# Spreading a norm's factors over the partitions through memory in a two-layer decoder trunk: two feed-forward norms on one Trainium2 core

## The chip, the cores and the metric

The kernel runs on one core of one Trainium2 chip. The metric is the device time of one execution in microseconds, lower is better, and the time of a kernel is the median of its runs. The engines named below are TensorE (PE for its matmuls, PEld for its weight loads), VectorE (DVE), ScalarE (ACT), GpSimd (POOL) and SyncE (SP). Each engine takes its instructions in program order, and the engines wait for one another only through semaphores.

## What is computed

A token stream x of 512 rows by 1024 features passes two layers. Each has a mixer (a convolution and pooling mixer in layer 0, attention in layer 1) and then a gated feed-forward part, which is what matters here:

```python
def rmsnorm(x, g):
    y = x32 * lax.rsqrt(jnp.mean(x32 * x32, axis=-1, keepdims=True) + EPS)
    return y * g
def conv_glu_ffn(xn, w_up, conv_w, conv_b, w_down):
    u = causal_dwconv3(xn @ w_up, conv_w) + conv_b
    gate, up = jnp.split(u, 2, axis=-1)          # 2816 columns each
    return (jax.nn.silu(gate) * up) @ w_down
x = x + conv_glu_ffn(rmsnorm(x, ffn_norm[layer]), ...)
```

The norm gives one factor for each token, `rsqrt(mean + EPS)`.

## The kernel before

**Layout.** Features lie on the 128 partitions and the 512 tokens along the free axis, so that x is 8 tiles of 128 x 512. Each float32 matrix product is made of three passes with the operands split into a rounded part and a rest (`wh`, `wl` for weights, `xh`, `xl` for x). A weight unit of 128 output columns is thus 8 x 3 = 24 matmuls of 128 x 512 (lines 1184 to 1186, in `product`). SP loads each unit from memory into one of four slots `raw`, ACT rounds it to `wh` (L483, `round_unit`, called by `ahead`), POOL subtracts to get `wl` (L448), and PE waits for that (`unit_ready`). ACT may round a unit only when PE is done with the unit four before it (`s_unit`), since they share a slot.

**The norm.** The gain is multiplied in before the product, but the token's factor is only applied after it: PE multiplies the raw x by the weights, and DVE multiplies the result in PSUM by `rstd` (L963), which must hold the 512 factors as a row, the same on all 128 partitions. The factors are made with tokens on partitions: ACT squares, DVE sums the squares into `acc`, four small matmuls (`norm_stats`, L1201) sum over the features and leave the means as a column of 4 values on each of the 128 partitions, and DVE works out the inverse root in twelve tiny steps (L835 to L838) into `small[:, 3, 0:4]`, which raises `s_rn`. Then PE spreads them: four transposes of a column repeated along the free axis (`norm_spread`, L1208) write 128 x 512 into the PSUM bank `nbank`, and ACT copies it to `rstd` (`keep_rstd`, L510), which DVE waits for.

**The order around the feed-forward part.** `first_two` makes units up and up + 1 together, tile of x by tile of x, as the tiles become ready. Then units up + 2 and up + 3 follow, then a loop over the rest, one unit after the other into four PSUM banks in turn; unit up + 4 writes bank 0 again, so PE waits there for DVE's first multiplication (`s_z`). In layer 0 the squares are ready in the midst of `first_two`: the statistics stand before its fifth tile and the spread before its eighth. In layer 1 (`late`) the statistics come after `first_two`, and the spread within unit up + 2, after five of its eight tiles. The DVE and ACT steps for the pair (gate, up) are in `hidden`: L963 for gate and up, L595 and L599 on ACT (scale and bias of the third tap), four fused multiply-adds L970 on DVE, then the silu L605 on ACT. In ACT's program the rounding of unit up + 4 stands between L595 and L599, and that of unit up + 5 right behind the first silu.

The kernel also uses memory as a go-between once already: 16 rows of bias are written by ACT's queue (L564), and each head loads one of them with an overlapping pattern into 128 partitions of 2 KB (L703).

## Time and profile before

| | |
|---|---|
| median of 3 runs | 1115.33 us (1115.22 to 1115.8) |
| the profiled execution's own time | 1115.61 us |
| its span in the trace | 1113.6 us |
| PE busy | 1107.0 us, 99% of the span |
| DVE, ACT, POOL busy | 53%, 45%, 42% |
| granted clock of TensorE | 1.00 |

The busy share of PE is modelled from pipelined matmuls; a stretch without a gap shows more surely in the starts of its matmuls in the timeline. A row of the timeline gives the start, the duration, the engine and line, the operation with its tiles, and in brackets how long the engine had been idle before and what ended that.

### The profile page before, as it was taken

To read this page: it belongs to the slowest core of one execution; us is meant where nothing else is said; L and a number is where in the kernel's file an instruction comes from. 1 tells how busy PE (TensorE), PEld (TensorE's weight loads), DVE (VectorE), ACT (ScalarE), POOL (GpSimd) and SP (SyncE) were. 2 spreads that over 40 slices of the span, in tenths; PEclk is the share of its full clock that TensorE was granted. 3 is DMA by queue.
4 is the path that set the end of the run, shared out by engine and by line. 5 is a ranking of instruction groups with operands and counts; after the bars stand their busy time and mean duration, and the time that the engine had idled before them with its cause. 6 is when DMAs were issued, how large, how long until landed. Compare 5 with 4: busy or idle time off the path is not lost.

```text
span 1113.6 us, 15736 instructions
## 1 busy us (share of the span) xinstructions
PE 1107.0 (99%) x5252; PEld 943.6 (85%) x5252; DVE 585.9 (53%) x1070; ACT 498.8 (45%) x805; POOL 462.6 (42%) x221
## 2 busy tenths in 40 slices
PE   9999999999999999999999999999999999999998
PEld 7788888888888888889999999888888888888887
DVE  6785755454454521125688888887654454540000
ACT  5333444444444423223777777644443444442120
POOL 4454534444445354543223233144544445344442
PEclk9999999999999999999999999999999999999999
DMA  8232313223232233333222333122323232224331
GB/s 270 76 115 86 123 59 112 100 88 113 78 111 85 64 104 100 96 94 118 76 77 76 102 98 95 49 98 91 120 87 113 79 109 94 78 66 116 90 107 72
DMA packets 47125, 108.19 MB, mean 97 GB/s; under 512 B 4272, under 2 KB 19632, under 8 KB 47088
## 3 DMA queue, kind: packets, MB, share of 16 engines
q1 hardware_dynamic: 44752, 103.46, 29.3%
q10 hardware_dynamic: 2336, 4.24, 1.5%
q8 instruction: 22, 0.36, 0.1%
q14 instruction: 15, 0.12, 0.0%
HBM read 105.54 MB, written 2.15 MB: 97 GB/s over the span
## 4 chain that ended last, share of the span: by engine, by line
issue 45%; PE 34%; POOL 20%; DMA 1%; SPq 1%; POOLq 0%; ACT 0%; DVE 0%; DVEq 0%
POOL wl L448 20%; PE bank L1184 7%; PE bank L1186 7%; PE bank L1185 7%; PE spt L1184 4%; PE spt L1186 4%; PE spt L1185 4%; DMA raw<-w_in 1%; SPq L377 0%; POOLq L447 0%; POOLq L453 0%; SPq L384 0%; PE obank L1186 0%; PE obank L1184 0%; PE obank L1185 0%
## 5 line engine op out<-in xcount | busy, mean ns | idle before, releaser
L448 POOL TENSOR_TENSOR wl<-raw,wh 128x1024 fp32r<-128x1024 f32 (+2 forms) x214 | 458.0, 2145 | 626.5 <-ACT wh L483 626.1
L1184 PE MATMUL bank<-xh,wh 128*128 128x512 f32 x800 | 311.9, 390 | 0.0
L1186 PE MATMUL bank<-xh,wl 128*128 128x512 f32 x800 | 311.4, 389 | 0.0
L1185 PE MATMUL bank<-xl,wh 128*128 128x512 f32 x800 | 311.3, 389 | 0.0
L483 ACT ACTIVATE wh<-raw 128x1024 fp32r<-128x1024 f32 (+2 forms) x214 | 201.9, 946 | 152.2 <-PE spt L1186 139.9
L963 DVE TENSOR_TENSOR work<-bank,rstd 128x512 f32<-128x512 f32 x88 | 60.6, 691 | 225.7 <-PE bank L1186 223.7
L1184 PEld LDWEIGHTS bank<-xh,wh 128*128 128x128 f32 x800 | 150.2, 188 | 31.8 <-issue 0.9
L1186 PEld LDWEIGHTS bank<-xh,wl 128*128 128x128 f32 x800 | 150.2, 188 | 31.2
L1185 PEld LDWEIGHTS bank<-xl,wh 128*128 128x128 f32 x800 | 150.2, 188 | 31.1
L1184 PE MATMUL spt<-bh,wh 128*128 128x512 f32 x440 | 171.5, 390 | 0.4 <-POOL wl L448 0.3
L1185 PE MATMUL spt<-bl,wh 128*128 128x512 f32 x440 | 171.3, 389 | 0.0
L1186 PE MATMUL spt<-bh,wl 128*128 128x512 f32 x440 | 171.2, 389 | 0.0
L970 DVE SCALAR_TENSOR_TENSOR work<-work,par 128x512 f32<-128x512 f32 x176 | 127.8, 787 | 2.4 <-ACT work L599 1.8
L935 DVE TENSOR_TENSOR x<-spt,x 128x512 f32 (+1 forms) x27 | 18.6, 690 | 208.0 <-PE spt L1186 208.0
L599 ACT ACTIVATE work<-work,par 128x512 f32<-128x512 f32 x44 | 35.9, 816 | 142.2 <-DVE work L963 142.2
L1184 PEld LDWEIGHTS spt<-bh,wh 128*128 128x128 f32 x440 | 82.6, 188 | 18.3 <-POOL wl L448 0.7
L1186 PEld LDWEIGHTS spt<-bh,wl 128*128 128x128 f32 x440 | 82.6, 188 | 17.1
L1185 PEld LDWEIGHTS spt<-bl,wh 128*128 128x128 f32 x440 | 82.6, 188 | 17.1
L1366 PE MATMUL bank<-wh,xh 128*128 128x384 f32 x256 | 87.6, 342 | 0.1
L1368 PE MATMUL bank<-wh,xl 128*128 128x384 f32 x256 | 85.7, 335 | 0.0
L1367 PE MATMUL bank<-wl,xh 128*128 128x384 f32 x256 | 85.7, 335 | 0.0
L595 ACT ACTIVATE work<-work,par 128x512 f32<-128x512 f32 x44 | 35.9, 817 | 57.6 <-DVE work L963 57.6
(154 smaller groups left out, 1140.8 us busy)
## 6 DMA issues: line engine op xcount, KB each, us to landing
raw<-w_up SPq DMA_DIRECT2D x88, 512.0 KB, 3.2
raw<-w_down SPq DMA_DIRECT2D x32, 384.0 KB, 3.1
raw<-w_qkv SPq DMA_DIRECT2D x32, 384.0 KB, 3.4
raw<-w_down SPq DMA_DIRECT2D x32, 320.0 KB, 2.9
raw<-w_in SPq DMA_DIRECT2D x14, 512.0 KB, 3.7
raw<-w_out SPq DMA_DIRECT2D x8, 512.0 KB, 3.2
work<-bias_rows ACTq DMA_DIRECT2D x16, 256.0 KB, 3.8
raw<-w_o SPq DMA_DIRECT2D x8, 512.0 KB, 3.3
```

What stands on the lines that cost most here:

```text
L448: nc.gpsimd.tensor_tensor(wl[s][:, 0:n], raw[s][:, 0:n], plain(wh[s][:, 0:n]), ALU.subtract).then_inc(s_lo, 1)
L483: nc.scalar.activation(wh[s][:, 0:n], raw[s][:, 0:n], ACT.Copy).then_inc(s_hi, 1)
L595: nc.scalar.activation(ug, zg[j][:, 2:], ACT.Identity, bias=col(i * 16 + (c + 3)), scale=col(i * 16 + (c + 2))).then_inc(s_id, 1)
L599: nc.scalar.activation(uu[j], zu[j][:, 2:], ACT.Identity, bias=col(i * 16 + (c + 7)), scale=col(i * 16 + (c + 6))).then_inc(s_id, 1)
L963: nc.vector.tensor_tensor(buf[:, 2:], bank[2 * j + n][:], rstd[:], ALU.mult).then_inc(s_z, 1)
L970: nc.vector.scalar_tensor_tensor(u, z[:, tap:tap + SEQ], col(i * 16 + (c + 4 * n + tap)), u, ALU.mult, ALU.add).then_inc(done, 1)
L1184: mm(dst, wh[s][:, w], hi, start=first, stop=False)
L1185: mm(dst, wh[s][:, w], lo, start=False, stop=False)
L1186: return mm(dst, wl[s][:, w], hi, start=False, stop=last)
L1366: mm(dst, xh[:, k, rows], pair_weights(wh, k), start=k == 0, stop=False)
L1367: mm(dst, xh[:, k, rows], pair_weights(wl, k), start=False, stop=False)
L1368: return mm(dst, xl[:, k, rows], pair_weights(wh, k), start=False, stop=k == KT - 1)
```

## The change

For the two feed-forward norms, the four transposes on PE and ACT's copy of their result are taken out. In their place ACT's queue writes the 4 x 128 factors to a row of 512 floats in memory (`rstd_rows`), waits until they have landed, and loads that row into all 128 partitions of `rstd`. DVE waits for the load. In ACT's program the rounding of unit up + 4 now stands ahead of these two transfers. The two mixer norms are left as they are.

```diff
+    rstd_rows = nc.dram_tensor("rstd_rows", [2, SEQ], F32, kind="Internal").ap()
...
             def ffn(layer, up, down):
-                keep = layer + 2
+                def send_rstd():
+
+                    act.wait_ge(s_rn, 2 * layer + 2)
+                    row = rstd_rows[layer:layer + 1, :]
+                    act.dma_start(row.rearrange("a (t q) -> (a q) t", q=P), small[:, 3, 0:TB],
+                                  allow_slow_non_contiguous=True).then_inc(s_row, 16)
+                    act.wait_ge(s_row, (layer + 1) * 16)
+                    src = bass.AP(tensor=row.tensor, offset=row.offset, ap=[[0, P], [1, SEQ]])
+                    act.dma_start(rstd[:], src).then_inc(s_rstd_in, 16)
...
                     ahead(up, i, 2 * j)
                     if first:
-                        keep_rstd(keep)
+                        ahead(up, i, 1)
+                        send_rstd()
                     act.wait_ge(s_z, f * 2 + 1)
...
-                    ahead(up, i, 2 * j + 1)
+                    if not first:
+                        ahead(up, i, 2 * j + 1)
...
-                dve.wait_ge(s_rstd, layer + 2)
+                dve.wait_ge(s_rstd_in, (layer + 1) * 16)
...
-                    if not late and k == KT - 1:
-                        norm_spread(norm)
...
                 if late:
                     norm_stats(norm)
-                    unit_ready(up + 2)
-                    up_part(2, 0, 5)
-                    norm_spread(norm)
-                    up_part(2, 5, KT).then_inc(s_unit, 1)
-                else:
-                    project(bank[2][:], up + 2, 2)
+                project(bank[2][:], up + 2, 2)
```

How this moves ACT's program at the start of layer 1's feed-forward part, in the kernel before. The first row is the rounding of unit up + 3, the third of unit up + 4, the last of unit up + 5:

```order
483 L483 ACTIVATE wh<-raw 128x1024 [waits s_unit,s_raw3]
484 L510 ACTIVATE rstd<-spt 128x512 [waits s_bc]
485 L595 ACTIVATE work<-work,par 128x512 [waits s_z]
486 L483 ACTIVATE wh<-raw 128x1024 [waits s_unit,s_raw0]
487 L599 ACTIVATE work<-work,par 128x512 [waits s_z]
488 L605 ACT_TABLE_LOAD
489 L605 ACTIVATE work<-work 128x512 [waits s_t0]
490 L483 ACTIVATE wh<-raw 128x1024 [waits s_unit,s_raw1]
```

The same place in the changed kernel, whose line numbers are a few higher (L486 is the rounding, L607 and L612 are what L595 and L599 were):

```order
484 L486 ACTIVATE wh<-raw 128x1024 [waits s_unit,s_raw3]
485 L486 ACTIVATE wh<-raw 128x1024 [waits s_unit,s_raw0]
486 L590 DMA rstd_rows<-small 128x4x1 [waits s_rn]
487 L594 DMA rstd<-rstd_rows 128x512 [waits s_row]
488 L607 ACTIVATE work<-work,par 128x512 [waits s_z]
489 L612 ACTIVATE work<-work,par 128x512 [waits s_z]
490 L618 ACT_TABLE_LOAD
491 L618 ACTIVATE work<-work 128x512 [waits s_t0]
492 L486 ACTIVATE wh<-raw 128x1024 [waits s_unit,s_raw1]
```

The rounding of unit up + 4 has moved ahead of everything that needs the factors; it now waits only for unit up. That of unit up + 5 still stands behind the silu, and so behind both transfers.

On PE, in layer 1, the kernel before has this in the midst of unit up + 2 (the last three matmuls of its fifth tile, the spread, the first of its sixth):

```order
2269 L1184 MATMUL bank<-xh,wh 128x512
2270 L1185 MATMUL bank<-xl,wh 128x512
2271 L1186 MATMUL bank<-xh,wl 128x512
2272 L1208 MATMUL spt<-par,small 128x128 [waits s_rn]
2273 L1208 MATMUL spt<-par,small 128x128 x3
2274 L1184 MATMUL bank<-xh,wh 128x512
```

In the changed kernel the same place is matmuls alone, and PE no longer waits for `s_rn`:

```order
2267 L1197 MATMUL bank<-xh,wh 128x512
2268 L1198 MATMUL bank<-xl,wh 128x512
2269 L1199 MATMUL bank<-xh,wl 128x512
2270 L1197 MATMUL bank<-xh,wh 128x512
2271 L1198 MATMUL bank<-xl,wh 128x512
```

## Rows read from the trace of the kernel before

**Rows 1.** The page: busy times, and the granted clock in 40 slices
```profile
span 1113.6 us, 15736 instructions
PE 1107.0 (99%) x5252; PEld 943.6 (85%) x5252; DVE 585.9 (53%) x1070; ACT 498.8 (45%) x805; POOL 462.6 (42%) x221
...
PEclk9999999999999999999999999999999999999999
```

**Rows 2.** Waits of PE over the whole span (us in total, times, longest)
```profile
PE bank L1247 <- DVE wh L855: 1.7, 1, 1.7
PE obank L1230 <- DVE gate L846: 0.9, 1, 0.9
PE spt L1184 <- POOL wl L448: 0.3, 1, 0.3
```

**Rows 3.** Timeline of PE, layer 0: the spread, and the starts of three units
```profile
153.89 0.60 PE L1208 MATMUL spt<-par,small 128*128 128x128 f32 x4
154.24 0.48 PE L1184 MATMUL bank<-xh,wh 128*128 128x512 f32 x1
...
161.16 0.39 PE L1184 MATMUL bank<-xh,wh 128*128 128x512 f32 x1
...
166.60 0.39 PE L1184 MATMUL bank<-xh,wh 128*128 128x512 f32 x1
...
172.04 0.39 PE L1184 MATMUL bank<-xh,wh 128*128 128x512 f32 x1
```

**Rows 4.** Timeline of PE, layer 1: unit up's end, spread, three units
```profile
759.69 0.39 PE L1186 MATMUL bank<-xh,wl 128*128 128x512 f32 x1
...
764.94 0.60 PE L1208 MATMUL spt<-par,small 128*128 128x128 f32 x4
...
767.45 0.39 PE L1184 MATMUL bank<-xh,wh 128*128 128x512 f32 x1
...
772.89 0.39 PE L1184 MATMUL bank<-xh,wh 128*128 128x512 f32 x1
...
778.33 0.39 PE L1184 MATMUL bank<-xh,wh 128*128 128x512 f32 x1
```

**Rows 5.** Timeline of ACT, layer 0's first pair
```profile
156.04 0.82 ACT L595 ACTIVATE work<-work,par 128x512 f32<-128x512 f32 x1 [0.92 <-DVE work L963]
```

**Rows 6.** Timeline of DVE: layer 0's first factors; layer 1's roots
```profile
155.32 1.29 DVE L963 TENSOR_TENSOR work<-bank,rstd 128x512 f32<-128x512 f32 x2 [2.60 <-PE bank L1186]
...
761.78 0.17 DVE L805 TENSOR_SCALAR guess<-small 128x4 int32<-128x4 int32 x1
...
763.77 0.17 DVE L838 SCALAR_TENSOR_TENSOR small<-small 128x4 f32<-128x4 f32 x1
...
766.26 1.29 DVE L963 TENSOR_TENSOR work<-bank,rstd 128x512 f32<-128x512 f32 x2 [1.93 <-issue]
```

**Rows 7.** Timeline of POOL: layer 1's unit up + 3, up + 4, up + 5
```profile
758.89 2.38 POOL L448 TENSOR_TENSOR wl<-raw,wh 128x1024 fp32r<-128x1024 f32 x1 [3.52 <-ACT wh L483]
768.83 2.39 POOL L448 TENSOR_TENSOR wl<-raw,wh 128x1024 fp32r<-128x1024 f32 x1 [7.56 <-ACT wh L483]
774.13 5.21 POOL L448 TENSOR_TENSOR wl<-raw,wh 128x1024 fp32r<-128x1024 f32 x2 [2.91 <-ACT wh L483]
```

**Rows 8.** Timelines of DVE and POOL: the attention norm's roots
```profile
513.61 1.70 DVE L805 TENSOR_SCALAR guess<-small 128x4 int32<-128x4 int32 x1
515.35 0.17 DVE L806 TENSOR_SCALAR small<-small 128x4 f32<-128x4 f32 x1
...
509.82 5.47 POOL L448 TENSOR_TENSOR wl<-raw,wh 128x768 fp32r<-128x768 f32 x3 [6.31 <-ACT wh L483]
```

**Rows 9.** Timelines of DVE, ACT, POOL: a later pair that nothing disturbs
```profile
189.77 2.73 DVE L970 SCALAR_TENSOR_TENSOR work<-work,par 128x512 f32<-128x512 f32 x4
...
191.87 0.63 ACT L605 ACTIVATE work<-work 128x512 f32<-128x512 f32 x1 [1.10 <-DVE work L970]
192.41 1.04 ACT L483 ACTIVATE wh<-raw 128x1024 fp32r<-128x1024 f32 x1
...
193.53 2.40 POOL L448 TENSOR_TENSOR wl<-raw,wh 128x1024 fp32r<-128x1024 f32 x1 [5.30 <-ACT wh L483]
```

**Rows 10.** DMA issues: KB each, median us from issue to landing
```profile
raw<-w_down SPq DMA_DIRECT2D x32, 384.0 KB, 3.1
raw<-w_qkv SPq DMA_DIRECT2D x32, 384.0 KB, 3.4
...
raw<-w_in SPq DMA_DIRECT2D x4, 256.0 KB, 5.4
...
bias_rows<-bv_sb ACTq DMA_DIRECT2D x1, 48.0 KB, 1.8
```

**Rows 11.** The sixteen bias loads (L703) alone: issue to landing
```profile
DMA to landing us min/median/max: 3.0/3.8/5.2
```

More of the change, by code:

```diff
@@ L236, in trunk @@
         s_rstd = sem("s_rstd")
+        s_row = sem("s_row")
+        s_rstd_in = sem("s_rstd_in")
         s_small = sem("s_small")
@@ L506, in prep, with keep_rstd @@
                 nc.scalar.activation(sq[:], tile(x, k), ACT.Square).then_inc(s_sq, 1)
-            def keep_rstd(spreads):
-                act.wait_ge(s_bc, spreads)
+            def keep_rstd():
+                act.wait_ge(s_bc, 1)
                 nc.scalar.activation(rstd[:], nbank, ACT.Copy).then_inc(s_rstd, 1)
@@ L548, in _ @@
                 if g == 0:
-                    keep_rstd(1)
+                    keep_rstd()
                 else:
@@ L1202, in norm_stats, with norm_spread @@
                 last.then_inc(s_ms, 1)
-            def norm_spread(norm):
-                pe.wait_ge(s_rn, norm + 1)
+            def norm_spread():
+                pe.wait_ge(s_rn, 1)
                 for b in range(TB):
@@ L1273, in _ @@
             first_end(2)
-            norm_spread(0)
+            norm_spread()
             first_end(3)
@@ L1313, in _ @@
                 project(rbank[n % 2], U_OUT + n, n % RING, bh, bl, MIX)
-            def up_part(j, k0, k1):
-                for k in range(k0, k1):
-                    last = product(bank[j][:], j, k, xh[:, k, :], xl[:, k, :], k == 0, k == KT - 1)
-                return last
             def ffn(layer, up, down):
```

## The prediction

> **What bounds the kernel now.** I read the page first: PE is busy in 1107.0 of 1113.6 us at full granted clock, no other engine above 53% [rows 1]. A busy share of pipelined matmuls proves little, so the list of PE's waits comes next: three waits, 2.9 us in all, two of them at the start, and none in a feed-forward part [rows 2]. Then the starts in PE's timeline: unit up + 3 of layer 0 begins at 161.16, the next at 166.60 and 172.04 [rows 3], that is 24 matmuls in 5.44 us, 227 ns each, and layer 1 shows the same from 767.45 to 772.89 to 778.33 [rows 4]. So the end is set by PE's own instructions in a row. Taking an instruction from PE gives its time back, and any other engine costs nothing until it comes later than PE needs it. The question is how much slack the factors have.
>
> **What is removed.** In layer 0 the spread begins at 153.89 and unit up + 2 begins six matmuls later. Unit up + 2 is one unit of 5.44 ahead of 161.16, so it begins at 155.72; six matmuls take 6 x 0.227 = 1.36, so the spread cost 155.72 - 153.89 - 1.36 = 0.47 us [rows 3]. In layer 1: from the spread at 764.94 to unit up + 3 at 767.45 are nine matmuls, 2.51 - 2.04 = 0.47 us [rows 4]. PE did not wait for `s_rn` at either place. Together **-0.94 us**. ACT's copy goes too; it lies beside PE.
>
> **What is added, and when PE would notice.** Two transfers in a row: W, the write of the factors until it has landed, and R, the load, each from issue to landing. The end of R starts DVE's first multiplication; call that time z. Two things of PE hang on z. Unit up + 4 needs bank 0 free, at z + 0.75. Unit up + 5 needs its weights, whose rounding stands behind the first silu on ACT. The second comes later, worked out so: L595 starts 0.72 behind z (155.32 to 156.04) and takes about 0.8 [rows 5, 6]; L599 follows at z + 1.5 and ends at z + 2.3; of the four fused steps the second needs it, so it and the third take until z + 3.7 at 2.73 / 4 = 0.68 each, and the silu starts at about z + 3.75. From the silu to the rounding is 0.54, from the rounding to POOL's start 1.12, and POOL takes 2.40 [rows 9]. PE can start unit up + 5 at **z + 7.9**. Before, this chain took longer, since POOL's work on unit up + 4 lay in its midst [rows 7]; the moved rounding takes that out of the way, which is why I don't take the old length.
>
> *Layer 0.* The factors are ready long before; ACT reaches the write when unit up is done, 0.47 earlier than DVE's start at 155.32 shows it, so the issue is at about 155.0, right behind the start of the moved rounding. z = 155.0 + W + R + 0.2. PE wants unit up + 5 at 172.04 - 0.47 = 171.57, so z may be as late as 163.7: no stall while W + R is under 8.5 us.
>
> *Layer 1.* Here the statistics come after `first_two`, and the moved rounding does harm. Unit up's last matmul starts at 759.69 and ends near 760.1 [rows 4]; ACT rounds unit up + 4 until 761.3, when POOL has just ended up + 3 (758.89 + 2.38 = 761.27) [rows 7]. POOL starts up + 4 then and holds to 763.7. DVE's twelve tiny steps run in this very time, from 761.6 [rows 6]. What happens is seen at the attention norm: the step L805 took 1.70 us in place of 0.17 and ended when POOL's run ended, 509.82 + 5.47 = 515.29 [rows 8]. So L805 at 761.78 ends at 763.7, not 761.95, and `s_rn` comes 1.76 later than 763.94, at 765.7 [rows 6]. The write goes out at 765.8, z = 766.0 + W + R. PE wants unit up + 5 at 778.33 - 0.47 = 777.86, so z may be 769.96 at most. **The stall is W + R - 3.96.**
>
> *W.* Nothing in the trace writes pieces of four bytes. The lower bound is the one write there is, 16 rows: 1.8 us [rows 10]. `small` holds each factor apart in memory order, so the write is 512 pieces. What pieces cost: the w_qkv load moves the same 384 KB as a w_down load in three pieces for each partition in place of one, and lands after 3.4 in place of 3.1 us [rows 10]. 256 pieces more for 0.3 us make 0.6 for some 500 more: 2.4. The only row with 512 pieces is a first w_in load, 5.4 us in a full queue [rows 10], which is the upper bound. I take 2.5, near the lower, since at that time one weight load at most is in flight.
>
> *R.* The bias loads have its shape, 128 rows of 2 KB from one small region of memory: 3.0 to 5.2, median 3.8 [rows 11]. The weight load that POOL's work on unit up + 4 releases at 763.7 is over when R starts, and the next one waits for unit up + 5, which is what is late; so R has the queues for itself. I take 3.2, near the shortest.
>
> W + R = 5.7, the stall in layer 1 is 1.7 us, and in layer 0 there is none (margin 2.8). The sum is -0.94 + 1.7 = **+0.8 us**. On the profiled execution's own 1115.61 (its span of 1113.6 and 2.0 around it) that is 1116.4; the median of the runs lies 0.28 lower, so I predict **1116.1**. A stall of this length should not cost more than itself: after PE's 1.7 us wait at the start the granted clock still reads full [rows 1, 2].
>
> The Trainium skill, "DMA: Bandwidth & Descriptors", Anatomy of one DMA, gives a fixed cost of about 2.0 us for each transfer plus its bytes over 436 GB/s, most of it the receipt of the write, memory being the slowest target. As an estimate from that page W is 2.0 and R 2.0 + 0.6 = 2.6, so that W + R would be 4.6, the stall 0.6 and the time 1115.0. That formula was fitted on GpSimd's path; the rows here, where the sum uses ACT's queue, lie above it for the load (3.0 at least) and below it for the write (1.8), so the sum goes by the rows. The same page, Rules for kernel authors, says that a last dimension that is not contiguous becomes one descriptor for each element; no run here shows it yet, and the 512 pieces above are counted from the code's strides.
>
> **The rivals.**
>
> 1. *The transfers are hidden, or nearly.* W at the bound 1.8 and R at 3.0 make 4.8: a stall of 0.84, time 1115.2. If besides DVE is not held up by POOL in layer 1, 1.76 goes from the stall and nothing is left: 1114.4. For it: both bounds are measured rows, and layer 0 has slack to spare. Against it: L805 was held up once in just this meeting [rows 8], and four-byte pieces can hardly be faster than rows of 3 KB in their fixed part. The page's formula above falls into this case.
> 2. *Slower than can be told from no change.* One mechanism: the round trip through memory in layer 1 is long, so that unit up + 5's weights come late. It decides from a stall of 3.2 us, W + R over 7.1. With R like the longest bias load, 5.2, and W 3.0, W + R is 8.2, the stall 4.2, and the time 1118.6; with R at the median 3.8 and W 5.4 it is 9.2, layer 0 stalls by 0.7 too, and the time is 1120.3. For it: W is unmeasured and all 128 partitions read the same 2 KB. Against it: the queues are nearly empty there.
> 3. *Faster by over 0.2%.* That needs 2.2 us. The removed work on PE is 0.94 in all, and PE waits for nothing around it [rows 2 to 4], so there is nothing more to gain.
>
> **How the numbers follow.** About 0.2%, 2.2 us, is what a measurement of this kernel can tell from no change: 1113.1 to 1117.5. The forecast (a stall between 0.84 and 3.1 us in layer 1, 1115.2 to 1117.5) has 0.60, rival 1 has 0.18, rival 2 has 0.20, rival 3 has 0.02. Forecast and rival 1 are within the bound, so faster 0.02, same 0.78, slower 0.20. The range runs from rival 1 without any stall, 1114.4, to rival 2's first price, 1118.6.
>
> **What the changed profile would show.** No transposes at the feed-forward norms, and starts of matmuls 227 ns apart through the place of the spread. In layer 0 a write issued near 155.0, z near 160.9, PE without a wait. In layer 1 the step that was L805 stretched to about 1.9 us under POOL, the write issued at 765.8, z at 771.7, POOL's unit up + 5 from about 777.1, and one wait of PE for POOL of about 1.7 us at the start of unit up + 5, none elsewhere. I am wrong if the wait is at bank 0 (then z is not followed by the chain of 7.9), if the write's landing takes over 4 us, if the roots run undisturbed beside POOL, or if PE waits in later pairs as well, which would mean that the lag is carried on rather than made up in DVE's idle time.

## The result, and the profile of the changed kernel

The changed kernel takes **1130.48 us** (median of 4 runs, 1130.01 to 1131.01) against 1115.28 us (1114.93 to 1115.8) for the kernel before on the same chip: 1.0135 times as long, 95% interval 1.0123 to 1.0147, 15.2 us slower. The forecast was 1116.1 with a range to 1118.6.

The page of the changed kernel, its busy line and the granted clock in 40 slices (before: [rows 1]):

```profile
span 1129.0 us, 15721 instructions
...
PE 1111.5 (98%) x5244; PEld 945.4 (84%) x5244; DVE 595.2 (53%) x1070; ACT 498.1 (44%) x803; POOL 463.7 (41%) x221
...
PEclk9999999999999999999999999998999999999999
```

The span is 15.4 us longer although PE has eight instructions fewer. A slice of the clock is below full for the first time, the 28th, which begins 27/40 into the span, at 762 us: layer 1's feed-forward part. PE's waits say where (before: [rows 2]; us in total, times, longest):

```profile
PE bank L1197 <- DVE work L976: 11.9, 2, 7.2
```

Two new waits, one in each layer, both for DVE's first multiplication by the factors (L976), which frees bank 0. In PE's timeline they stand at unit up + 4. Layer 0 (before: [rows 3]), the end of unit up + 3, unit up + 4's first two matmuls, the first that is quick again, and the first of up + 5:

```profile
165.43 0.39 PE L1199 MATMUL bank<-xh,wl 128*128 128x512 f32 x1
170.49 0.79 PE L1197 MATMUL bank<-xh,wh 128*128 128x512 f32 x1 [4.67 <-DVE work L976]
171.07 0.63 PE L1198 MATMUL bank<-xl,wh 128*128 128x512 f32 x1
...
173.52 0.40 PE L1198 MATMUL bank<-xl,wh 128*128 128x512 f32 x1
...
177.52 0.50 PE L1197 MATMUL bank<-xh,wh 128*128 128x512 f32 x1
...
777.80 0.39 PE L1199 MATMUL bank<-xh,wl 128*128 128x512 f32 x1
785.42 0.79 PE L1197 MATMUL bank<-xh,wh 128*128 128x512 f32 x1 [7.24 <-DVE work L976]
786.01 0.63 PE L1198 MATMUL bank<-xl,wh 128*128 128x512 f32 x1
...
791.13 0.43 PE L1198 MATMUL bank<-xl,wh 128*128 128x512 f32 x1
...
793.71 0.39 PE L1197 MATMUL bank<-xh,wh 128*128 128x512 f32 x1
```

The rows from 777.80 on are the same place in layer 1 (before: [rows 4]). Every microsecond is in these rows. After the first matmul behind the wait they start 0.43 us apart where it was 0.227 before, until the spacing returns to 0.23 (from the 8th matmul in layer 0, from the 14th in layer 1). Layer 0 lost 170.49 - (165.43 + 0.23) = 4.83 us waiting, and unit up + 4 took 177.52 - 170.49 = 7.03 us in place of 5.44, 1.59 more. Layer 1 lost 785.42 - 778.03 = 7.39 and 8.29 - 5.44 = 2.85. That is 12.22 of waiting and 4.44 of slow matmuls, 16.66 in all. Against the kernel before, unit up + 5 starts 5.48 us later in layer 0 (177.52 for 172.04) and 15.38 later in layer 1 (793.71 for 778.33), and 15.38 is the whole difference of the spans. So 1.28 us came back elsewhere: 0.94 for the transposes and 0.34 of small shifts. The largest of these is 0.47 us by which this execution was ahead before layer 0's feed-forward part (the statistics' matmuls start at 148.40, before at 148.87).

This is what each stretch took, not what each cause cost. The slow matmuls are for the most part not lost on top: POOL had the weights of unit up + 5 ready only 7.9 us behind DVE's first multiplication, at 177.5 and about 792.5, and at full clock PE would have stood still until then. Measured so, they cost next to nothing in layer 0 (177.52) and 1.2 us in layer 1 (793.71).

What DVE waited for is in ACT's timeline of both places, where the queue's instructions have "ACTq":

```profile
154.38 0.40 ACTq L590 DMA_DIRECT2D rstd_rows<-small  x1
165.50 0.34 ACTq L594 DMA_DIRECT2D rstd<-rstd_rows  x1
170.39 0.81 ACT L607 ACTIVATE work<-work,par 128x512 f32<-128x512 f32 x1 [14.97 <-DVE work L976]
...
771.35 0.38 ACTq L590 DMA_DIRECT2D rstd_rows<-small  x1
779.85 0.34 ACTq L594 DMA_DIRECT2D rstd<-rstd_rows  x1
```

Between the write's issue and the load's lie 11.1 and 8.5 us. The load may only be issued once the write has landed, so this is the write's landing. The trace's list of DMA issues (KB each, median us to landing; before: [rows 10]) has it as the slowest transfer of the kernel, with no more than 2 KB to move:

```profile
raw<-w_up SPq DMA_DIRECT2D x88, 512.0 KB, 3.3
...
rstd<-rstd_rows ACTq DMA_DIRECT2D x2, 256.0 KB, 4.4
...
bias_rows<-bv_sb ACTq DMA_DIRECT2D x1, 48.0 KB, 1.8
rstd_rows<-small ACTq DMA_DIRECT2D x2, 2.0 KB, 9.8
```

The same view over 154.3 to 166 us alone, 40 slices of 0.29 us (share of the 16 DMA engines in tenths, and GB/s), then packets by queue and landings:

```profile
DMA  0003400000000000340000005631901430202350
GB/s 0 0 0 3 4 0 0 0 0 0 0 0 0 0 0 0 84 140 0 0 0 0 0 0 42 56 14 70 70 0 28 28 28 14 28 0 28 28 42 0
...
q10 hardware_dynamic: 528, 0.00, 2.2%
...
raw<-w_up SPq DMA_DIRECT2D x1, 512.0 KB, 10.6
rstd<-rstd_rows ACTq DMA_DIRECT2D x1, 256.0 KB, 4.1
rstd_rows<-small ACTq DMA_DIRECT2D x1, 2.0 KB, 11.1
```

All packets of ACT's queue, 528 for the 512 pieces, pass in the fourth and fifth slice, 155.2 to 155.8 us. Then nothing moves for 3 us, and the write counts as landed at 165.5. The landing is not made of time in which the DMA engines are shown busy. A weight load issued by SP at 158.07 starts, stops for some 2 us and trickles at 14 to 70 GB/s; it lands after 10.6 us where its kind takes 3.3.

The Trainium skill, "DMA: Bandwidth & Descriptors", Anatomy of one DMA, says of GpSimd's path that a transfer's semaphore is raised only when the last byte is confirmed in the target memory, and that this receipt is most of a fixed cost of about 2 us. By that the order of events in the trace, packets first and the landing long behind, is what is to be expected; the size is not, since from the last packet to the landing it took 7 to 10 us here. Its Rules for kernel authors say that a strided last dimension becomes one descriptor for each element; the trace agrees, with 528 packets for 512 elements.

### The profile page after: what moved, and what is told of

It reads as the page before. It is cut to its first block, busy times and chain, and to the rows that moved or that the text cites. A ratio compares the mean times of both kernels' runs of the same rounds, so it can differ in the third digit from the quotient of the medians.

```text
span 1129.0 us, 15721 instructions
## 1 busy us (share of the span) xinstructions
PE 1111.5 (98%) x5244; PEld 945.4 (84%) x5244; DVE 595.2 (53%) x1070; ACT 498.1 (44%) x803; POOL 463.7 (41%) x221
## 4 chain that ended last, share of the span: by engine, by line
issue 45%; PE 33%; POOL 19%; DMA 1%; POOLq 0%; DVE 0%; SPq 0%; ACT 0%; DVEq 0%
POOL wl L451 19%; PE bank L1197 7%; PE bank L1198 7%; PE bank L1199 7%; PE spt L1197 4%; PE spt L1199 4%; PE spt L1198 4%; DMA raw<-w_in 1%; POOLq L450 0%; SPq L380 0%; POOLq L456 0%; DVE guess L818 0%; PE obank L1198 0%; PE obank L1197 0%; PE obank L1199 0%
## 5 line engine op out<-in xcount | busy, mean ns | idle before, releaser
L486 ACT ACTIVATE wh<-raw 128x1024 fp32r<-128x1024 f32 (+2 forms) x214 | 202.0, 946 | 160.9 <-PE spt L1199 139.9
L976 DVE TENSOR_TENSOR work<-bank,rstd 128x512 f32<-128x512 f32 x88 | 60.3, 690 | 233.9 <-PE bank L1199 203.7
L983 DVE SCALAR_TENSOR_TENSOR work<-work,par 128x512 f32<-128x512 f32 x176 | 131.1, 806 | 0.6 <-ACT work L607 0.6
L612 ACT ACTIVATE work<-work,par 128x512 f32<-128x512 f32 x44 | 35.9, 815 | 131.2 <-DVE work L976 131.2
L607 ACT ACTIVATE work<-work,par 128x512 f32<-128x512 f32 x44 | 35.9, 816 | 85.2 <-DVE work L976 85.2
```

The source lines that it names most:

```text
L486: nc.scalar.activation(wh[s][:, 0:n], raw[s][:, 0:n], ACT.Copy).then_inc(s_hi, 1)
L607: nc.scalar.activation(ug, zg[j][:, 2:], ACT.Identity, bias=col(i * 16 + (c + 3)), scale=col(i * 16 + (c + 2))).then_inc(s_id, 1)
L612: nc.scalar.activation(uu[j], zu[j][:, 2:], ACT.Identity, bias=col(i * 16 + (c + 7)), scale=col(i * 16 + (c + 6))).then_inc(s_id, 1)
L976: nc.vector.tensor_tensor(buf[:, 2:], bank[2 * j + n][:], rstd[:], ALU.mult).then_inc(s_z, 1)
L983: nc.vector.scalar_tensor_tensor(u, z[:, tap:tap + SEQ], col(i * 16 + (c + 4 * n + tap)), u, ALU.mult, ALU.add).then_inc(done, 1)
```

## The experiments

### The two places apart, and the moved rounding alone

`layer0_only` and `layer1_only` make the change in one layer and keep the transposes in the other (shown for layer 0; the other has `layer == 1`):

```diff
-                    if first:
+                    by_row = layer == 0
+                    if first and by_row:
                         ahead(up, i, 1)
                         send_rstd()
+                    elif first:
+                        keep_rstd(2)
```

> The change in layer 0 alone; layer 1 keeps its four transposes and its order. By the starts of PE's matmuls in the changed kernel, layer 0 lost 6.4 us to the wait and to the slow clock behind it and gained 0.47. Theory (the two layers' losses add up): 1115.3 + 6.4 - 0.5 = 1121.2, 1120.5 to 1122. Rival (the loss is tied to something both share, such as code loading or a queue that is set up once): near 1115 or near 1130.

Measured: 1120.97 us (4 runs) against 1115.96, ratio 1.005 (1.0033 to 1.0067). The write landed after 9.4 us, the load after 4.3. PE's waits:

```profile
PE bank L1203 <- DVE work L982: 3.2, 1, 3.2
PE bank L1203 <- POOL wl L451: 1.3, 1, 1.3
```

> The change in layer 1 alone; layer 0 keeps its transposes and its order. By the starts of matmuls in the changed kernel layer 1 lost 10.2 us (7.4 waiting, 2.9 by the slow clock behind it) and gained 0.47. Layer 0 alone came to 1121.0 beside 1116.0. Theory: 1115.3 + 10.2 - 0.5 = 1125, 1124 to 1126, and the two parts together make the 15 us of the change. Rival: the losses do not add up, and one layer alone is worth under 8 or over 12 us.

Measured: 1123.86 us (4 runs) against 1115.08, ratio 1.0079 (1.0062 to 1.0096); write 7.4 us, load 4.3. PE's new wait:

```profile
PE bank L1203 <- DVE work L982: 5.9, 1, 5.9
```

5.0 and 8.8 us make 13.8 of the 15.2. The intervals, nearly 2 us to either side of each, leave room for two places that don't touch one another; the landing was 1.7 and 1.1 us shorter in these kernels than in the changed one, which would account for a difference too. After the 3.2 us wait in `layer0_only` the granted clock stayed at 1.00; behind the 5.9 us in `layer1_only` it was 0.50 from 778.5 to 782.5 us. `layer0_only` shows both of the waits that I had worked out: bank 0 first, then POOL's rest for unit up + 5, at full clock.

`moved_only` keeps the transposes and only rounds unit up + 4 earlier, in both layers:

```diff
                     if first:
+                        ahead(up, i, 1)
                         keep_rstd(keep)
...
-                    ahead(up, i, 2 * j + 1)
+                    if not first:
+                        ahead(up, i, 2 * j + 1)
```

> The kernel before with the rounding of unit up + 4 moved ahead of ACT's copy of the factors, and nothing else: four transposes in each layer, no transfers. Theory (the moved rounding only makes POOL hold up the twelve small steps of layer 1 by 1.8 us, and this is hidden, but PE itself waits at the spread for the roots): in layer 1 the roots are ready at about 765.8 and PE comes to the spread at 764.9, so PE waits 0.9 to 1.0 us: 1116.2. In layer 0 nothing waits: the copy of the factors is one microsecond later. Rival (no loss, since the small steps run undisturbed): 1115.3.

Measured: 1116.25 us (10 runs) against 1115.96, ratio 1.0003 (0.9994 to 1.0013), no difference that can be told. PE waited 0.7 us for the end of the roots, and DVE's timeline shows why, the step held up by POOL's work:

```profile
761.46 1.96 DVE L807 TENSOR_SCALAR guess<-small 128x4 int32<-128x4 int32 x1
```

So the moved rounding delays the roots, as forecast, and by itself costs a wait of 0.7 us in the trace; the runs alone bound it only at 1.5 us.

### The same bytes in other pieces

`piece16` writes the row in the order of `small`, four factors of a partition side by side, so that the write is 128 pieces of 16 bytes in place of 512 of 4. DVE's multiplication then reads `rstd` with a stride:

```diff
-                    act.dma_start(row.rearrange("a (t q) -> (a q) t", q=P), small[:, 3, 0:TB],
-                                  allow_slow_non_contiguous=True).then_inc(s_row, 16)
+                    act.dma_start(row.rearrange("a (q t) -> (a q) t", t=TB), small[:, 3, 0:TB]).then_inc(s_row, 16)
...
-                        nc.vector.tensor_tensor(buf[:, 2:], bank[2 * j + n][:], rstd[:],
+                        nc.vector.tensor_tensor(buf[:, 2:].rearrange("p (t q) -> p t q", t=TB),
+                                                bank[2 * j + n][:].rearrange("p (t q) -> p t q", t=TB),
+                                                rstd[:].rearrange("p (q t) -> p t q", t=TB),
```

> The changed kernel with the row in memory in the order of partitions (factor of token t * 128 + q at place 4 q + t), so that each partition writes one piece of 16 bytes, 128 in place of 512; the load is as before, and DVE reads rstd with a stride of 4. Theory (the write's landing is what costs, and it grows with the number of pieces): W falls to about 3 us, W + R to 7.2, so that layer 0 has no stall and layer 1 stalls by about W + R - 3.96 = 3.2 us: 1115.3 - 0.9 + 3.2 = 1117.6, between 1115.5 and 1119. Rival (the write is slow because memory is the target, whatever its pieces): W stays at 8 to 11 and the time at 1128 to 1131. Rival (a strided read of rstd makes DVE slow): L976's mean rises from 0.69 us and PE waits in the later pairs.

Measured: 1116.3 us (10 runs, 1115.86 to 1118.05) against 1115.96, ratio 1.0004 (0.9994 to 1.0013), span 1113.8. The load and the write in the list of DMA issues:

```profile
rstd<-rstd_rows ACTq DMA_DIRECT2D x2, 256.0 KB, 3.6
...
rstd_rows<-small ACTq DMA_DIRECT2D x2, 2.0 KB, 1.8
```

The one wait of PE in a feed-forward part:

```profile
PE bank L1198 <- POOL wl L451: 1.5, 1, 1.5
```

The form of the write takes nearly all of the 15 us away. What is left is the kernel that the prediction described: one wait, 1.5 us, at the start of unit up + 5 in layer 1, for POOL. One term differs, though: DVE's two strided multiplications took 2.05 us in place of 1.29, and unit up + 5 starts 8.5 us behind the first of them (769.93 to 778.40) where the prediction has 7.9.

`pieces4_by_partition` separates size from order. The bytes stand in memory as in `piece16`, but their source lies apart, so that each 16 bytes go as four pieces of 4 (DVE leaves its factors in `apart`; the strided multiplication is that of `piece16`):

```diff
+        apart = sb("apart", [P, 2 * TB])[:].rearrange("p (t a) -> p t a", a=2)[:, :, 0]
...
-                    act.dma_start(row.rearrange("a (t q) -> (a q) t", q=P), small[:, 3, 0:TB],
+                    act.dma_start(row.rearrange("a (q t) -> (a q) t", t=TB), apart,
```

> The kernel with the row in the order of partitions, but written in 512 pieces of 4 bytes as the change does (DVE leaves the four factors of a partition 8 bytes apart, so that they can't be joined). Number and size of the pieces, and 16 of them for each 64 bytes, are those of the change; only here they come from four neighbouring partitions in place of sixteen. Theory 'pieces for each 64 bytes': the write takes 8 to 11 us and the time is 1124 to 1130. Rival 'many engines on 64 bytes': the write takes 2 to 3 us, and the time is about 1117.

Measured: 1126.42 us (4 runs) against 1115.08, ratio 1.0099 (1.0082 to 1.0115). The write in its list of DMA issues, which PE paid for with two waits at bank 0, 7.0 us in all:

```profile
rstd_rows<-apart ACTq DMA_DIRECT2D x2, 2.0 KB, 7.1
```

Same memory, same order, same load, same multiplication: four-byte pieces cost 7.1 in place of 1.8 us and bring the slow kernel back. So the order of the factors in memory is not what makes the write slow. It may still have a part in how slow: the change's own order landed after 9.8 us in the median and took 4 us more in all, while alone, as shown below, both orders take 8.3.

`shifted16` is `piece16` with the row begun 16 bytes later:

```diff
-    rstd_rows = nc.dram_tensor("rstd_rows", [2, SEQ], F32, kind="Internal").ap()
+    rstd_rows = nc.dram_tensor("rstd_rows", [2, SEQ + 16], F32, kind="Internal").ap()
...
-                    row = rstd_rows[layer:layer + 1, :]
+                    row = rstd_rows[layer:layer + 1, 4:4 + SEQ]
```

> The kernel with 128 pieces of 16 bytes, which ran at 1116.3 us with a write of 1.5 to 2.0 us, with nothing changed but that the row in memory begins 16 bytes further on. Number, size and order of the pieces and the load are the same, but each 64 bytes of memory now hold partitions 4n + 3 to 4n + 6, from two groups of four. Theory 'engines' (64 bytes of memory written from two DMA engines): the write's landing is back at about 8 us, W + R at 12, and the time at 1124 to 1129. Rival 'pieces' (what counts is how many pieces there are, or how small): the write stays at 1.5 to 2 us and the time at 1116.3.

Measured: 1116.43 us (10 runs) against 1115.29, ratio 1.0006 (0.9997 to 1.0016); write 1.6 to 1.7 us, load 3.8. The theory that a write is slow when its pieces share 64 bytes with those of another DMA engine falls for pieces of 16 bytes.

### Which writes are slow

The first of these kernels put one extra write of one shape after another into the kernel before, on ACT's queue at places where ACT has time. Its idea and two of its shapes:

```diff
+            def probe(kind):
+                if probes:
+                    act.wait_ge(s_probe, 16 * len(probes))
...
+                if kind == "a":
+                    dma = act.dma_start(pr["a"].rearrange("(t q) a -> q (t a)", q=P), src, allow_slow_non_contiguous=True)
...
+                if kind == "e":
+                    dma = act.dma_start(pr["e"], par[:, 0:1], allow_slow_non_contiguous=True)
```

> The kernel before, with extra writes on ACT's queue that nothing in the computation waits for, two of each shape, each alone in flight on that queue, read by their time from issue to landing. Shapes, all from a constant tile: a) 512 pieces of 4 bytes side by side in memory, as the change writes them; b) 128 pieces of 16 bytes; c) the 512 pieces 64 bytes apart; d) 512 bytes apart; e) 128 pieces of 4 bytes side by side; f) 128 pieces of 64 bytes; g) 512 pieces of 4 bytes with an SBUF tile as target; h) 4 pieces of 512 bytes. Theory 'lines': single 4-byte writes into the same line of memory wait for one another, because memory can only rewrite a line whole. Then a is 8 to 11 us, e is between 3 and 6, b is 3 to 4, c, d, f, g and h are 1.8 to 3. Rival 'count': each small write to memory costs its time wherever it goes. Then a, c and d are alike at 8 to 11, b, e and f alike at about 3.5 (a quarter of the pieces), g and h near 2. Rival 'descriptors': making and running 512 descriptors is slow whatever the target. Then g is 8 to 11 as well. Rival 'place': the write is slow only beside weight loads at the head of the feed-forward part. Then all shapes are 2 to 3 except where a weight load is in flight, and the two instances of one shape differ by more than the shapes do.

Measured: 1115.29 us (one run), no wait of PE above 0.9 us. All shapes shared one semaphore here, so the landings are worked out from its events: shape a, the 512 side-by-side pieces, 8.7 to 9.5 us; b, 16-byte pieces, 2.1 and 3.2; c and d, one element for each 64 and 512 bytes, 1.8 to 3.4; e, 128 pieces of 4 bytes side by side, 8.0 and 8.1; f, 64-byte pieces, 1.4 and 3.0; g, to SBUF, 2.6 and 3.8; h, 4 pieces of 512 bytes, 1.2 and 1.3. The number of pieces alone is thus not what counts: c has as many as a, and e a quarter of them.

The second gave every write its own semaphore and varied the distance between single four-byte elements of 128 partitions:

```diff
+                if kind == "s4":
+                    dma = act.dma_start(pr[i][0:0 + P * 1].rearrange("(q a) -> q a", a=1)[:, 0:1], par[:, 0:1], allow_slow_non_contiguous=True)
+                if kind == "s8":
+                    dma = act.dma_start(pr[i][0:0 + P * 2].rearrange("(q a) -> q a", a=2)[:, 0:1], par[:, 0:1], allow_slow_non_contiguous=True)
```

> The kernel before with seventeen extra writes on ACT's queue, each with its own semaphore and each alone in flight there, read by the time from issue to landing. The first such kernel showed the slow ones at about 8 to 9.5 us, 512 pieces of 4 bytes side by side and 128 such pieces alike, and the 512 pieces 64 bytes apart at 2 to 3; what is open is whether a line of 64 bytes is slow because it gets many pieces, or because its pieces come from different DMA engines. The Trainium skill, DMA: Bandwidth & Descriptors, The descriptor swizzle, gives four neighbouring partitions to each engine. Shapes: 128 pieces of 4 bytes with a pitch of 4, 8, 16, 32 and 64 bytes (16, 8, 4, 2 and 1 pieces for each 64 bytes, from 4, 2, 1, 1 and 1 groups of four partitions); 128 pieces of 16 bytes side by side, unshifted, and with the whole shifted by 16 bytes and by 32 (4 pieces for each 64 bytes in all three, from 1, 2 and 2 groups); 128 pieces of 64 bytes, unshifted and shifted by 32 bytes; 512 pieces of 4 bytes side by side, 64 bytes apart, and into SBUF. Theory 'engines': slow, 8 us, are the pitches 4 and 8 and the shifted 16-byte pieces, and the shifted 64-byte pieces too; fast, 1.5 to 3 us, are the pitches 16, 32, 64 and everything unshifted. Rival 'pieces for each line': the time falls step by step from pitch 4 to 64 (8, 5, 3, 2, 2) and the shift of the 16-byte pieces changes nothing, 2 us.

Measured: 1115.47 us (one run). The elements side by side landed after 7.4 and 8.0 us, the 16-byte pieces after 1.4; the issue cost 0.33 us in both. Elements 8 bytes apart landed after 2.9 and 3.1 us, 16 to 64 apart after 2.9 to 3.2. The change's own shape took 10.0 and the 512 pieces 64 bytes apart 3.3; 16-byte pieces begun 16 bytes later took 3.9 and 1.8, and begun 32 bytes later 3.2. Some of these had other transfers beside them, which is why the next kernels leave the whole computation out and keep only writes, each waited for before the next:

```diff
+                def done(dma, k):
+                    dma.then_inc(s_k[k], 16)
+                    act.wait_ge(s_k[k], 16 * (r + 1))
...
+                done(act.dma_start(mem["tq"][r][0:SEQ].rearrange("(t q) -> q t", q=P), four, allow_slow_non_contiguous=True), "tq")
...
+                done(act.dma_start(mem["tq64"][r][0:16 * SEQ].rearrange("(t q a) -> q t a", q=P, a=16)[:, :, 0], four, allow_slow_non_contiguous=True), "tq64")
```

> The transfers by themselves: all computation is left out (the output is a copy of the input), and ACT's queue makes one transfer after the other, each waited for before the next, nothing else in flight, four times each. 128 pieces of 4 bytes with a pitch of 4, 8, 16, 32, 64, 128; pieces of 8 bytes side by side; of 16 side by side, shifted by 16 bytes, and 64 apart; 512 pieces of 4 bytes by token (the change's: neighbours in memory are neighbouring partitions), by partition (64 bytes come from four partitions), and 64 bytes apart; 16 pieces from 16 partitions into the same 64 bytes, and 64 bytes apart; 512 pieces into SBUF; two loads, 128 rows of 2 KB from the same 2 KB and from memory of their own. Theory 'pieces for each 64 bytes': the time grows with how many writes meet in 64 bytes, whoever makes them: 16 side by side are 7 to 8 us by token, by partition and for the 16 pieces alone, and it falls with the pitch (8 bytes: 3 to 4, 16: 2 to 3, 64: 1.5). Rival 'many engines on 64 bytes': by partition is 2 to 3 us although 16 pieces meet there, by token is 8, and the 16 pieces alone, on 16 engines, are 7 or more. Loads: if the shared row is what made the load take 4.1 to 4.7 us, it is over 1 us slower than rows of their own; if not, both are near 2.5 to 3.

Measured (233.44 us for the whole kernel with its four rounds): the changed kernel's write, L183, and the 16-byte pieces, L180:

```profile
L183 ACTq DMA_DIRECT2D m_tq<-gap x4: 377/378/378, 40.0 to 200.8; - x4
...
DMA to landing us min/median/max: 8.3/8.3/8.3
...
L180 ACTq DMA_DIRECT2D m_e<-gap x4: 326/326/327, 35.2 to 195.8; - x4
...
DMA to landing us min/median/max: 1.4/1.4/2.1
```

The last kernel asks how many neighbours it takes, and whether they must come from different partitions:

```diff
+                done(act.dma_start(mem["n16"][r][0:16].rearrange("(q a) -> q a", a=1)[:, 0:1], gap[0:16, 0:1], allow_slow_non_contiguous=True), "n16")
...
+                done(act.dma_start(mem["own4"][r][0:16 * P].rearrange("(q a) -> q a", a=16)[:, 0:4], apart4, allow_slow_non_contiguous=True), "own4")
```

> Again the transfers by themselves (all computation left out), four times each. The last such kernel left this open: 128 pieces of 4 bytes side by side took 6.9 us, with a pitch of 8 bytes 4.1, of 16 bytes 1.7, yet 16 pieces side by side in one 64 bytes only 1.3, so it isn't simply the number of writes that meet in 64 bytes. Shapes: 16, 32, 64 and 128 partitions with 4 bytes each side by side (1, 2, 4, 8 pieces for each of the 16 DMA engines); 32, 64 and 128 with a pitch of 8; 64 with a pitch of 16; 512 pieces as four side by side of each partition in 64 bytes of its own; 256 as two side by side; 512 pieces 16 bytes apart, four for each partition; 2048 pieces, sixteen side by side of each partition; 256 pieces of 8 bytes, two side by side of each partition. Theory 'one engine, one small block': writes that one engine makes into the same 16 to 32 bytes wait for one another. Then 16 is 1.3, 32 is 2 to 3, 64 and 128 are 4 to 7; four side by side in memory of their own are as slow as the change's write, 8 us, and 16 bytes apart they take 2 to 3. Rival 'neighbours from other partitions': four side by side from one partition, in 64 bytes of its own, are fast, 2 to 3 us, and only the rows where partitions share 64 bytes are slow. Rival 'total': the time follows the number of pieces under 8 bytes whatever their place; then 16 bytes apart is 8 too.

Measured (246.15 us): 128 elements side by side, L178, and 512 with the four of each partition side by side in 64 bytes of its own, L183:

```profile
L178 ACTq DMA_DIRECT2D m_n<-gap x4: 350/350/353, 26.5 to 198.7; - x4
...
DMA to landing us min/median/max: 7.0/7.2/7.5
...
L183 ACTq DMA_DIRECT2D m_own<-gap x4: 388/388/394, 45.9 to 217.8; - x4
...
DMA to landing us min/median/max: 2.5/3.0/3.4
```

All small writes of these two kernels, medians of four in us, nothing beside them:

| write to memory | pieces | landing |
|---|---|---|
| 4 bytes, side by side, token order (the change) | 512 | 8.3 |
| the same, partition order (7.0 to 9.5) | 512 | 8.3 |
| 4 bytes, side by side, many per partition | 2048 | 13.9 |
| 4 bytes, side by side | 128 | 6.9, 7.2 |
| 4 bytes, side by side | 64 / 32 / 16 | 6.6 / 3.0 / 1.3 |
| 4 bytes, 8 bytes apart | 128 | 4.1, 3.6 |
| 4 bytes, 8 bytes apart | 64 / 32 | 3.5 / 3.8 |
| 4 bytes, 16 bytes apart | 128 / 64 | 1.7 / 1.6 |
| 4 bytes, 32, 64 or 128 bytes apart | 128 | 1.4 |
| 4 bytes, 64 bytes apart | 512 / 16 | 2.0 / 1.3 |
| 4 bytes, 16 bytes apart, four of each partition in a row | 512 | 3.8 |
| 4 bytes, each partition's four side by side in its own 64 | 512 | 3.0 |
| the same with two in each partition | 256 | 2.0 |
| 8 bytes, side by side | 128 | 3.0 |
| 8 bytes, side by side, two per partition | 256 | 3.9 |
| 16 bytes, side by side; 64 bytes apart | 128 | 1.4; 1.4 |
| 16 bytes, side by side, begun 16 bytes later | 128 | 1.6 |
| 4 bytes, 8 bytes apart in SBUF, four in each partition | 512 | 2.0 |

Payload and issue explain none of it, and the number of pieces only in part: 512 pieces 64 bytes apart land in 2.0 us, 64 side by side in 6.6, but among pieces side by side the landing grows from 1.3 us for 16 of them to 13.9 for 2048. What the slow writes share is pieces of 4 or 8 bytes close together in memory, and the closer they lie the later they land. What happens there stays open, and each theory that the two kernels were built for fails on a row. "So much for each piece that shares 64 bytes" fails, since 16 pieces in one 64 bytes take 1.3. "Slow only where many DMA engines meet in 64 bytes" fails, since partition order, where each 64 bytes come from four partitions, is as slow as token order. "One engine, one small block" would have four side by side of one partition as slow as the change's write, and they take 3.0. "The number of small pieces wherever they lie" would have 512 of them 16 bytes apart near 8, and they take 3.8. The last rival, that only neighbours from other partitions count, fares best, but these four still cost 1.0 more than spread ones, four of one partition 16 bytes apart 1.8 more, and shifted 16-byte pieces hardly anything.

### What was to be had

`no_spread` leaves the spreading of the two feed-forward norms out altogether:

```diff
                         ahead(up, i, 1)
-                        send_rstd()
...
-                dve.wait_ge(s_rstd_in, (layer + 1) * 16)
+                dve.wait_ge(s_rn, 2 * layer + 2)
```

> The changed kernel without the two transfers: the feed-forward parts multiply by the factors that the first mixer norm left in rstd, so their own factors are worked out and left out of the result. This is what the removal of the transposes alone is worth, with the rounding moved as in the change. Theory: 0.94 us less than before, 1114.4. Rival (the transposes cost PE more than the starts of the matmuls show, or removing PE's wait for the roots moves something else): below 1113 or not below 1115.

Measured: 1114.53 us (11 runs) against 1115.29, ratio 0.9993 (0.9983 to 1.0002), span 1112.8 for 1113.6. The gain of a spread that costs nothing at all is thus the 0.8 us of the span, near the 0.94 of the sum, and can't be told from no change by the runs.

`early16` is `piece16` with the rounding of unit up + 4 moved once more, between the write and the wait for its landing. It is then behind the roots and no longer meets them:

```diff
+                    ahead(up, 0, 1)
                     act.wait_ge(s_row, (layer + 1) * 16)
...
                     if first:
-                        ahead(up, i, 1)
                         send_rstd()
```

> The kernel with 128 pieces of 16 bytes, with the write issued ahead of the rounding of unit up + 4 and the load behind it. What is left of a loss in that kernel is one wait of PE for POOL of 1.5 us in layer 1, and there POOL held up the twelve small steps by 1.8 us. Theory: without the rounding ahead of them the roots are ready 1.8 us earlier, the wait is gone, PE has only the 0.94 us less of the transposes, and the time is 1114.4 to 1114.8 beside a before of 1115.3. Rival (the load meets the weight load and is late by as much): the wait stays and the time is 1116.

Measured: 1114.48 us (11 runs, 1114.08 to 1116.94) against 1115.29, ratio 0.9992 (0.9983 to 1.0001). Its list of PE's waits has none in a feed-forward part, and its root step takes its 0.17 us:

```profile
762.59 0.17 DVE L817 TENSOR_SCALAR guess<-small 128x4 int32<-128x4 int32 x1
```

It is the best version. Its profiled execution took 1115.98 us, above the median, so that its span of 1114.1 us says nothing against it; but the interval holds 1. No version was found that is surely faster.

## Why the prediction was wrong

**The step that failed** is the price of the write: "256 pieces more for 0.3 us make 0.6 for some 500 more: 2.4 ... I take 2.5, near the lower". It measured 11.1 and 8.5 us. The step priced pieces as work of the DMA engines, from loads whose pieces are a kilobyte, and in this it was even right: the 528 packets passed in 0.6 us. What takes the time comes behind the packets, between the last of them and the landing, where four-byte pieces lie side by side in memory, and no row of the kernel before has such a write. My upper bound, 5.4 from a load of 512 pieces, bounded the wrong thing too. Against that `piece16` shows 2.0 and 1.5 us for the same bytes, about my lower bound of 1.8. The landing over 4 us was on my own list of signs of being wrong.

**The load** was taken at 3.2, near the shortest bias load, with the queues to itself. It took 4.1 and 4.7, 3.4 and 3.8 in `piece16`, and 3.2 with nothing else on the chip's queues. Mis-sized by 0.9 and 1.5 us. That it had the queues to itself was right in layer 1, where no other packet passes from 773 to 785 us, and there it took the longest; so company is not the cause. In all four kernels with a slow write the loads behind it took 4.0 to 4.7 us, in the three with 16-byte pieces 3.2 to 3.9. Why is open.

**The formulas held where their terms are put in.** Layer 0: a stall of W + R - 8.5 = 11.1 + 4.1 - 8.5 = 6.7; unit up + 5 stood at 177.52, 5.95 behind the 171.57 at which PE wanted it, and the write went out 0.6 earlier than the formula's 155.0. Layer 1: 8.5 + 4.7 - 3.96 = 9.2. With the transposes' -0.94 this makes +15.0; measured were +15.2. The sum is nearer than its parts, and in part by luck: layer 0 came to 5.95 for 6.7, as the write went out early, and layer 1 to 10.4 for 9.2, as slow matmuls that no formula had came on top. z + 7.9 stands in the trace of layer 0 to the tenth: 169.66 + 7.9 = 177.56.

**Bank 0 bound first.** The prediction named it as one of the two things that hang on z and as a sign of being wrong. With z this late, z + 0.75 is past the time at which PE wants unit up + 4, so that PE stands still there. At full clock unit up + 4 then takes 5.44 us, and PE waits once more for unit up + 5, as in `layer0_only` (3.2 and 1.3 us). With slow matmuls in unit up + 4 the second wait is filled. In layer 0 both chains end together; in layer 1 the slow matmuls made unit up + 4 end 1.2 us behind z + 7.9 (784.60 + 7.9 = 792.5 for 793.71).

**The clock.** "A stall of this length should not cost more than itself" was said of 1.7 us, from one row. In the traces 1.5 us in `piece16` and 3.2 us in `layer0_only` left the granted clock at 1.00, but a wait of 1.9 us at bank 0 in layer 0 of `pieces4_by_partition` was followed, from the fourth matmul on, by eight that start 0.4 us apart, at a granted clock of 0.50. So the sentence held for `piece16`, and the length of the stall alone does not decide it; in the runs of `layer0_only` that have no kept trace the mean clock over the span read 0.997 or 0.998, so that it may have fallen there. In the changed kernel the slow matmuls cost 1.2 us beyond the chain of z + 7.9, all in layer 1.

**What was right.** The removed transposes (0.8 of span in `no_spread`, 0.94 in the sum). The step held up by POOL in layer 1, forecast at about 1.9 us from [rows 8]: here is DVE's timeline in the changed kernel (before: [rows 6]), the step before it, the step, and the first multiplication after 13 us of waiting:

```profile
767.19 0.16 DVE L848 TENSOR_SCALAR small<-spt 128x4 f32<-128x4 f32 x1 [2.85 <-PE spt L1214]
767.39 1.96 DVE L818 TENSOR_SCALAR guess<-small 128x4 int32<-128x4 int32 x1
...
784.60 0.69 DVE L976 TENSOR_TENSOR work<-bank,rstd 128x512 f32<-128x512 f32 x1 [12.88 <-issue]
```

POOL's timeline (before: [rows 7]) has the work that held it up, two units in a row until 764.51 + 4.81 = 769.32, and then nothing for 20 us:

```profile
764.51 4.81 POOL L451 TENSOR_TENSOR wl<-raw,wh 128x1024 fp32r<-128x1024 f32 x2 [3.52 <-ACT wh L486]
789.98 5.20 POOL L451 TENSOR_TENSOR wl<-raw,wh 128x1024 fp32r<-128x1024 f32 x2 [20.66 <-ACT wh L486]
```

`piece16` bore out the rest of the forecast chain: a write issued at 764.55 (765.8 in the forecast, which did not count layer 0's transposes nor an early start), one wait of 1.5 us for POOL at unit up + 5, and no wait later. That 1.5 lies so near the forecast 1.7 is partly chance, since W + R was 5.3 there and the chain behind it longer. Rival 2 was the right mechanism in this, that the round trip through memory is too long, and was given 0.20; it had layer 1's wait at unit up + 5 in place of bank 0, its worst price, 1120.3, took W at 5.4, and the stated range left even that price out. The estimate from the Trainium skill that stood in rival 1, W + R of 4.6, fits `piece16` (1.8 + 3.6 = 5.4) within a microsecond and misses the change by 10.6 and 8.6.

## What to carry to other kernels

When a column with one element per partition goes to memory, don't let the elements land side by side one by one: give each partition 16 contiguous bytes, the smallest piece that was quick here, and absorb the order in the reader, as `piece16` does with a stride on DVE. Price a small write by its landing, not by its bytes or packets, and where the trace has no write of that piece size the upper bound is unknown, not the nearest load. And before a change that puts a round trip through memory in place of half a microsecond on the busiest engine, compare what it can give (0.94 us here) with the slack that it must fit into (8.5 and 4.0 us).

## What the runs showed of the hardware that was not expected

- Four-byte writes side by side in memory land after 6.6 to 8.3 us with 64 to 512 pieces, while their packets pass in under 1 us; 16-byte pieces of the same row take 1.4, and 512 four-byte pieces into SBUF, 8 bytes apart, 2.0. The cause in the memory path is open, and so is why the landing was 11.1 and 8.5 us in the changed kernel, 9.4 and 7.4 in the kernels with one of the two places, and 8.3 alone.
- Such a write holds up others. In layer 0 of the changed kernel, of `layer0_only` and of `pieces4_by_partition` a weight load of 512 KB was issued 3.7 us behind the write and took 10.6, 9.2 and 7.5 us; at the same place and distance in `piece16` it took 3.5. In the kernel with `s4`, where nothing waits for the 128 elements side by side, the weight loads issued 4.3 us behind them took 7.1 and 6.7. Each of these five landed 3.2 to 3.6 us behind the write. The same load in `layer0_only`, `piece16` and the kernel with `s4`:

```profile
raw<-w_up SPq DMA_DIRECT2D x1, 512.0 KB, 9.2
...
raw<-w_up SPq DMA_DIRECT2D x1, 512.0 KB, 3.5
...
raw<-w_up SPq DMA_DIRECT2D x1, 512.0 KB, 7.1
```

- In the waits of PE of 4.8 and 7.4 us the granted clock fell to its 1.2 GHz level, and behind them matmuls started 0.43 us apart in place of 0.227, for the first 7 and 13 of them. After waits of 1.5 and 3.2 us it stayed at 2.4 GHz in the profiled executions, yet after one of 1.9 us in `pieces4_by_partition` it fell. Windows of the changed kernel (stretch, us, busy time and instructions of PE, PEld, DVE, ACT, POOL, granted clock, DMA share, GB/s):

```profile
170.00:174.00 4.00, 3.51 (x10) 2.81 (x11) 3.71 (x7) 3.41 (x5) 0.00 (x0) 0.58 0.00 0
174.00:178.00 4.00, 4.00 (x18) 3.06 (x17) 4.00 (x5) 3.33 (x5) 2.95 (x2) 1.00 0.00 0
...
780.00:785.00 5.00, 0.00 (x0) 0.00 (x0) 0.40 (x1) 0.00 (x0) 0.00 (x0) 0.59 0.27 52
785.00:790.00 5.00, 4.58 (x11) 3.62 (x12) 4.71 (x8) 4.48 (x6) 0.02 (x1) 0.50 0.02 3
```

And behind the 3.2 us of `layer0_only`, then the 1.9 us of `pieces4_by_partition`, whose first matmul starts at 168.16:

```profile
169.00:173.00 4.00, 3.72 (x16) 3.10 (x17) 3.71 (x7) 3.62 (x5) 0.00 (x0) 1.00 0.00 0
...
169.00:172.00 3.00, 3.00 (x9) 2.32 (x8) 2.78 (x6) 2.76 (x4) 0.00 (x0) 0.50 0.00 0
```

- Loading one shared row of 2 KB into 128 partitions took 3.2 us, loading 128 rows of their own 2.6, both with nothing beside them.
- A multiplication on DVE that reads `rstd` with a stride of 16 bytes took 2.05 us for two in place of 1.29 [rows 6].
